# Turning the next head's queries and keys in four single steps instead of two double ones

## The reference, cut to what matters

```
def causal_block_attention(q, k, v, log_forget_cum=None):
    for i in range(seq // Q_BLOCK):                      # 8 blocks of 128 queries
        q_lo, q_hi = i * Q_BLOCK, (i + 1) * Q_BLOCK
        qb, kb, vb = q[:, q_lo:q_hi], k[:, :q_hi], v[:, :q_hi]
        s = einsum(qb, kb) * scale                       # (+ c_q - c_k in the forgetting attention)
        p = softmax(where(mask, s, NEG_INF))
        outs.append(einsum(p, vb))
```

## Time and profile before

| what | value |
|---|---|
| median of three runs | 1670.12 us |
| profiled execution | 1672.04 us, its span 1670.2 us |
| granted TensorE clock over the span | 0.962 of full speed |
| TensorE busy | 1525.2 us, 91% |
| VectorE busy | 939.5 us, 56% |
| ScalarE busy | 621.9 us, 37% |
| GpSimd busy | 124.4 us, 7% |
| forgetting attention | about 237 to 379 us of the span |
| latent attention | about 517 to 661 us of the span |

### The profile page before, as it was taken

The page is one execution under the profiler, slowest core; times in us unless marked ns, Lnnn a source line. Parts: engine busy times, 40 slices in busy tenths (PEclk is TensorE's granted clock), DMA queues, the critical chain, the costliest instruction groups (busy, mean ns, idle before and its releaser), DMA issues. The chain is left out here.

```text
span 1670.2 us, 19124 instructions
## 1 busy us (share of the span) xinstructions
PE 1525.2 (91%) x7214; PEld 1267.3 (76%) x7214; DVE 939.5 (56%) x1290; ACT 621.9 (37%) x1013; POOL 124.4 (7%) x104
## 2 busy tenths in 40 slices
PE   5999999987998888886799988999999999999999
PEld 4899877775577777674677766888888888888887
DVE  3310345666276664873582447888877787533433
ACT  4310224542313544212351325555555555323222
POOL 1000150002031001200220000000000000000000
PEclk9899999998998998997899998999999999999999
DMA  5130121004022001310655111223222231544743
GB/s 190 47 117 1 57 84 43 26 26 141 12 76 70 26 26 37 97 40 13 231 172 202 76 51 51 89 84 93 76 89 76 80 98 63 208 141 143 252 138 140
DMA packets 126502, 153.66 MB, mean 92 GB/s; under 512 B 11531, under 2 KB 94398, under 8 KB 126142
## 3 DMA queue, kind: packets, MB, share of 16 engines
q1 hardware_dynamic: 126224, 152.40, 27.8%
q10 hardware_dynamic: 189, 0.08, 0.0%
HBM read 115.55 MB, written 36.31 MB: 91 GB/s over the span
## 5 line engine op out<-in xcount | busy, mean ns | idle before, releaser
L489 PE MATMUL ps<-split_arena 128*128 128x512 f32 x1152 | 299.1, 413 | 25.3 <-ACT plain_arena L524 8.6
L1720 PE MATMUL ps<-split_arena 128*128 128x512 f32 x1320 | 308.9, 391 | 5.2 <-DVE split_arena L2166 3.5
L1720 PEld LDWEIGHTS ps<-split_arena 128*128 128x128 f32 x1320 | 248.0, 188 | 58.1 <-DVE split_arena L2166 4.0
L489 PEld LDWEIGHTS ps<-split_arena 128*128 128x128 f32 x1152 | 221.6, 198 | 74.4 <-issue 21.5
L1809 PE MATMUL ps<-down_w,down_a 128*128 128x512 f32 x352 | 137.0, 389 | 0.1
L1811 PE MATMUL ps<-down_w,down_a 128*128 128x512 f32 x352 | 136.9, 389 | 0.0
L1810 PE MATMUL ps<-down_w,down_a 128*128 128x512 f32 x352 | 136.9, 389 | 0.0
L1782 DVE TENSOR_TENSOR down_a<-plain_arena,down_a 128x1024 fp32r<-128x1024 f32 x44 | 53.9, 1225 | 143.7 <-ACT down_a L1771 143.7
L1720 PE MATMUL ps<-up_b,split_arena 128*128 128x512 f32 x528 | 129.7, 396 | 4.9 <-DVE split_arena L1648 4.9
L1720 PEld LDWEIGHTS ps<-up_b,split_arena 128*128 128x128 f32 x528 | 101.3, 192 | 26.6 <-DVE split_arena L1648 5.2
L1771 ACT ACTIVATE down_a<-plain_arena 128x1024 fp32r<-128x1024 f32 x44 | 46.7, 1061 | 161.3 <-PE ps L1811 141.8
(11 more groups left out here) (333 smaller groups left out, 2453.6 us busy)
## 6 DMA issues: line engine op xcount, KB each, us to landing
plain_arena<-scr_act SPq DMA_DIRECT2D x44, 512.0 KB, 3.6
plain_arena<-in_w_in SPq DMA_DIRECT2D x24, 512.0 KB, 4.2
scr_gate<-plain_arena SPq DMA_DIRECT2D x48, 256.0 KB, 2.0
plain_arena<-scr_gate SPq DMA_DIRECT2D x24, 512.0 KB, 4.2
plain_arena<-in_w_up SPq DMA_DIRECT2D x22, 512.0 KB, 5.2
up_raw<-in_w_up SPq DMA_DIRECT2D x22, 512.0 KB, 5.2
scr_act<-plain_arena SPq DMA_DIRECT2D x22, 512.0 KB, 2.6
plain_arena<-in_w_down SPq DMA_DIRECT2D x44, 256.0 KB, 3.9
```

The costliest lines, as they stand in the source:

```text
L489: mm = nc.tensor.matmul(m.ps[:, self.banks[half], :], w[:, k, :], src[:, k, h * BANK:(h + 1) * BANK], start=(j == 0), stop=(j == self.PER_ ...
L1720: mm = nc.tensor.matmul(o, self.w[j][w][:, k, :], self.h[j][k][h], start=(j in self.OPENS and k == 0 and n == 0), stop=(k == self.HK - 1 a ...
```

## The change

Each fill of q or k of a head now has a step of its own: q half 0 of the next head at i = 4, k half 0 of the next head at i = 6, then q half 1 of the head itself at its i = 0 and k half 1 at its i = 1. Only the two first halves stand ahead of an attention's first score. A score waits only for the half of the keys that it reads last: `self.at["k", h, i // 4] + 1`. ScalarE's copy of q half 0 waits for the scores of the present head's first four blocks only; the others wait for all the scores of the head before. The list of fills changes accordingly, and the three engines go through a step's q or k fill at the same place as before: after the score or the maximum that is issued in the step, and before the fills of P on TensorE and ScalarE.

```
-        fills = [(w, 0, half) for w in "qk" for half in range(2)]
+        fills = [("q", 0, 0), ("k", 0, 0)]
         for s in range(ATT_STEPS):
-            h, i = divmod(s, TT)
-            if h + 1 < H and i in (5, 6):
-                fills += [("qk"[i - 5], h + 1, half) for half in range(2)]
-            fills += [("p", s, a, min(4, i + 1 - a)) for a in range(0, i + 1, 4)]
+            fills += self.turned_in(s)
+            fills += [("p", s, a, min(4, s % TT + 1 - a)) for a in range(0, s % TT + 1, 4)]
+        self.at = {f: n for n, f in enumerate(fills)}
+
+    def turned_in(self, s):
+        h, i = divmod(s, TT)
+        which = {0: ("q", h, 1), 1: ("k", h, 1), 4: ("q", h + 1, 0), 6: ("k", h + 1, 0)}
+        return [which[i]] if i in which and which[i][1] < H else []
+
+    def qk_fills(self, s):
+        return [self.at[x] for x in self.turned_in(s)]
...
     def score(self, pe, s):
-        pe.wait_ge(self.lo, self.upto["k", h])
+        pe.wait_ge(self.lo, self.at["k", h, i // 4] + 1)
...
     def tensor(self, pe):
-        for what in "qk":
-            for f in self.fills_of(what, 0):
-                self.turn(pe, f)
+        for f in range(2):
+            self.turn(pe, f)
...
-            if not last and i in (5, 6):
-                for f in self.fills_of("qk"[i - 5], h + 1):
-                    self.turn(pe, f)
+            for f in self.qk_fills(s):
+                self.turn(pe, f)
...
     def split_hi(self, act, f):
         elif x[1]:
-            act.wait_ge(self.scores, TT * x[1])
+            act.wait_ge(self.scores, TT * (x[1] - 1) + (4 if x[0] == "q" and x[2] == 0 else TT))
```

More of the change, by code:

```diff
@@ L655, in tensor @@
         for s in range(ATT_STEPS):
-            h, i = divmod(s, TT)
-            last = h + 1 == H
-            if i == 7 and not last:
+            i = s % TT
+            if i == 7 and s + 1 < ATT_STEPS:
                 self.score(pe, s + 1)
@@ L730, in scalar @@
     def scalar(self, act):
-        for what in "qk":
-            for f in self.fills_of(what, 0):
-                self.split_hi(act, f)
+        for f in range(2):
+            self.split_hi(act, f)
         self.exponent(act, 0)
         for s in range(ATT_STEPS):
-            h, i = divmod(s, TT)
+            i = s % TT
             if s + 1 < ATT_STEPS:
@@ L787, in vector @@
     def vector(self, dve):
-        for what in "qk":
-            for f in self.fills_of(what, 0):
-                self.split_lo(dve, f)
+        for f in range(2):
+            self.split_lo(dve, f)
         self.maximum(dve, 0)
@@ L804, in vector @@
                 self.maximum(dve, s + 2)
-            if not last and i in (5, 6):
-                for f in self.fills_of("qk"[i - 5], h + 1):
+            if s < ATT_STEPS:
+                for f in self.qk_fills(s):
                     self.split_lo(dve, f)
```

## The result

| | before | changed kernel |
|---|---|---|
| median | 1670.29 us (8 runs) | 1677.06 us (8 runs) |
| profiled execution | 1672.04 us | 1681.84 us |
| mean granted clock over the timed runs | 0.9633 (29 runs) | 0.9629 (8 runs) |

The ratio of the times is 1.005, 95% interval 1.0037 to 1.0062: slower, by 6 to 10 us. The forecast was 1688.0, +17.9. The direction and the range held; the size was more than twice too large.

A forecast was written before the change was run, and what follows sets the result against it. TensorE, 91% busy, was taken as bound by pauses at head boundaries (turn, ScalarE copy, VectorE subtraction and their queues) and its clock. Boundaries +9.2, starts -0.8, clock +9.5 made +17.9: 1688.0 us, range 1676 to 1695.

The forecast's parts named there:

- i=4, +1.64: Step i=4: P's second turn waits for q's subtraction behind the maximum, so gate matmuls start 1.64 us later.
- i=5 and 6, zero over i=4 to 6: Steps i=5 and 6: fewer turns and a vanished 1.13 us pause offset i=4's 1.64 and 1.96 idle before k.
- i=0, +0.30: Next head's i=0: q's second half costs 0.4 and P waits for a later subtraction; gate matmuls 0.30 us later.
- i=1 and 2, a boundary +1.5 in all: k's second half delays i=2's score and P; with earlier shifts a boundary costs +1.5 us, six +9.2.
- Starts, -0.8: Both attention starts: second halves cost 1.6 us, fewer early turns win 0.34 (forgetting) and 2.04 (latent), sum -0.8.
- Clock: Behind the k turn at i=6: one clock fall at each of six boundaries, 1.6 us a fall, +9.5 us.
- rival (a): Boundaries: the same waits but no new clock falls, +8.4 us, 1678.5; chance 0.20.
- Rival (b): Boundaries: clock falls last twice as long, as at the attention's start, +27 us, 1697; chance 0.10.
- Rival (c): i=4 and i=6: q and k subtracted before P's second turn, pauses vanish, -18.5 us with starts, 1652; chance 0.08.
- Rival (d): New and old waits cancel and the clock holds, within 3 us of 1670; chance 0.04.

The follow-up runs named there:

- e3: Changed kernel with q's first half turned at i=3 and not at i=4: 1669.53 us, ratio 1.0001 to the kernel before.
- e1: Kernel before with only the changed start of each attention, head boundaries as before: 1668.18 us, ratio 0.9988 to the kernel before.
- e2: Kernel before with only the changed head boundaries, all four turns still ahead of the first score: 1679.43 us, ratio 1.0056 to the kernel before.
- e6: Changed kernel with q's first half at i=3 and ScalarE's copy of k's second half ahead of the output copy: 1664.96 us, ratio 0.9969 to before.
- e9: Changed kernel with four fewer gate matmuls ahead of the pause at i=6, making that pause longer: 1691.28 us, ratio 1.0133 to before.
- e10: Changed kernel with the gate matmuls of i=6 and 7 ahead of P's transposes: 1665.66 us, ratio 0.9974 to before.
- e5: Changed kernel with gate matmuls dealt out anew, seven more at i=5: 1663.61 us, ratio 0.9962 to before.
- e7: e6 with gate matmuls dealt out as in e5 and, at i=6 and 7, issued ahead of P's transposes: 1643.80 us, ratio 0.9830 to before.
- the mends: The two edits of e6 to the changed kernel: q's first half at i=3, k's second-half copy ahead of the output copy; together 1664.96 us.
- e8: Kernel before, q and k turned as before, with gate matmuls dealt out and moved as in e7: 1657.37 us, ratio 0.9924 to before.

## Why the prediction was wrong in size, point by point

- **i=4, +1.64**: right. Measured +1.63, by the wait that was named (the fifth tile of P for q's subtraction behind the maximum); e3 takes it away.
- **i=5 and 6, zero over i=4 to 6**: near. The row of the last head told where k would be turned (3.74 behind the maximum; 3.65 now), and -1.78 was measured against the -1.64 reckoned. The sentence that laid VectorE's differences aside, "now and afterwards alike", was harmless for the waits and not for the clock: it hid that the pause before k is 1.49 and not 1.87 at four of the six boundaries.
- **i=0, +0.30**: right to 0.01. The 0.15 us to the release, for which the prediction named no row, came out as 0.15 (VectorE's subtraction ends at 313.52, the transpose starts at 313.67).
- **i=1 and 2, a boundary +1.5 in all**: the place was right, the size was over. The score starts 1.16 late and not 1.44 (with the real shift of that place taken off, k's copy began 0.2 us sooner than reckoned, and from copy to release took 1.37 and not 1.46), its closing mask matmul 1.27, and P's own old wait behind it was swallowed, which gives 0.07 to 0.54 back. A boundary costs 1.17 on average, six 7.0 and not 9.2: a term over by 2.2. (By its own numbers the prediction's last step there, 287.07 and 1.54 against 287.04, makes 1.57 and not 1.54, 0.2 us more in the sum.)
- **Starts, -0.8**: -1.8 in the profiled execution, where the forgetting attention's stretch at low clock was also half as long as before; -0.2 in e1, where it was not. The DMA that hides the forgetting attention's gain was named rightly. Waits and starts together are then 7.0 - 0.2 = +6.8. That this is the measured difference of the medians, too, is in part chance: e2, the boundaries alone, lost 9.5 by its median, 2.5 more than their waits.
- **Clock, "I take a fall at each of six boundaries: +9.5"**: this step failed. The place was right (behind k's turn), and so was the price of most falls (1.4 to 1.6 us). The number was not: 13 of 30 in the traces with these pauses, three in the profiled execution. At the prices measured, those 13 make about 4 us for six boundaries (an estimate), and e2's median is 2.5 above its waits: either way less than half of 9.5. Over the whole program even less came out: a mean clock of 0.9629 (8 runs) beside 0.9633 (29 runs) is under 2 us more at half speed, and three groups of runs of the kernel before differ by as much among themselves (0.9633, 0.9629, 0.9631). In the one traced execution of each kernel the low stretches at the forgetting attention's start (6.8 us before, 3.4 after) and between the attentions (20.5 and 17.1) were shorter after the change; whether that is usual isn't known. Behind the step stood two last heads of one execution, both with a fall; in 14 last heads of seven executions it was 10. A thing that comes in some executions only was counted as one that always comes, and a pause of 1.49, at four of the boundaries, as one of 1.96.

What is left is rival (a), "the same waits, no new falls", to which 0.20 was given: +8.4 and 1678.5 by its sum, 1677.06 measured. The size that it forecast is partly luck, for its waits were over by 1.6 us and some falls came. Rival (b) had its form in single boundaries of e2 and e6, with a stretch of 6.8 us each, and in e9, where longer pauses gave falls at all places and two of them double; as a forecast for all six it was wrong. The rule of the Trainium skill that stands beside it (TensorE: Matmul & The Clock Gate, PE-mode transpose), that transposes do not count for the clock as other matmuls do, is neither shown nor contradicted by these runs. e10 has the same transposes with gate matmuls among them, and one fall at six boundaries beside 13 in 30; but it also takes away a pause, and one in six is no clear difference. Rival (c), faster than before, was wrong as the change stands, and its mechanism appeared nowhere: q's and k's subtractions never ran ahead. The time fell below the kernel before only with other edits (e5, e6, e7, e10). Rival (d) needed the score of i=2 not to wait; it waits 0.58.

Open: why a given fall comes or not in one execution. What goes with the pauses, and with the gate work in front of them, is its frequency. No experiment was made on the starts' stretches at low clock.

## What to carry to other kernels

Where fills of a shared ring are reordered, look for the consumer two fills later and for what stands ahead of the subtraction on the engine that frees the bank: moving a fill beside a step with two fills of its own costs a wait of that engine's whole queue, beside a step with one it costs only its work. A pause that another engine's chain sets is free room: put independent matmuls there, ahead of the waiting instruction (21 us here on top of the mends, 13 on double turns; the order of the turns with both mends gave 5). When a falling clock is part of a sum, take its frequency from as many places and executions as there are, from pauses of the length at hand, and don't set it at one.

## What the runs showed that was not expected

- The clock falls more often the longer the pause: at none of 12 boundaries behind 0.4 to 0.8 plus 1.06 us, at 5 of 20 behind 1.49 plus 0.97, at 8 of 10 behind 1.87 plus 0.97, and at all eight of e9, whose first pause is 2.4 us or more.
- A mean clock doesn't give the time: e1 had 0.9668 over its 12 runs against 0.9633 before, some 12 us less at low clock, and was 1.8 us faster, within its noise. That a fall costs little where TensorE stands still anyway would explain it, and the three falls at 0.9 us, which have the second pause inside them, point that way; no run here tests it.
- Step by step, where no fall stands, the shifts of one boundary repeat to 0.02 us from one execution to the next (the changed kernel and e2), so that sums of them can be forecast to a few microseconds, e7's for one (e8's was missed by 2 to 4); the spread of a kernel's runs (1659 to 1673 us in e1) is not in them.
